# Gate products from rounded parts, with the first one-hot on Pool

## The reference

```python
cand_i = (i1[..., :, None] * N_KEYS + i2[..., None, :])
top_s, pos = lax.top_k(cand_s, PEER_TOPK)
experts = jnp.take_along_axis(cand_i, pos, axis=-1)
gates = jax.nn.softmax(top_s, axis=-1)
u = expert_down[experts]
vv = expert_up[experts]
act = jax.nn.gelu(jnp.einsum("thkd,td->thk", u, hb), approximate=False)
return jnp.einsum("thk,thkd->td", (gates * act).astype(vv.dtype), vv)
```

## Time and profile before

| | |
|---|---|
| median of 3 runs | 1893.9 us (1893.64 to 1896.47) |
| profiled execution | 1895.4 us, its span 1893.7 us |
| PE busy | 1662.7 us, 88% |
| DVE busy | 1340.0 us, 71% |
| ACT busy | 859.2 us, 45% |
| Pool busy | 231.4 us, 12% |
| mean granted TensorE clock | 0.927 |
| gate products L1407, 512 records | 67.8 us, 275 ns each |
| one-hots L1540, 256 | 55.4 us, 278 ns each |
| gated one-hots L1543, 256 | 70.9 us, 339 ns each |

### The profile page before, as it was taken

The page is one execution under the profiler, slowest core; times in us unless marked ns, Lnnn a source line. Parts: engine busy times, 40 slices in busy tenths (PEclk is TensorE's granted clock), DMA queues, the critical chain, the costliest instruction groups (busy, mean ns, idle before and its releaser), DMA issues. The chain is left out here.

```text
span 1893.7 us, 26367 instructions
## 1 busy us (share of the span) xinstructions
PE 1662.7 (88%) x10148; PEld 1500.5 (79%) x10148; DVE 1340.0 (71%) x2454; ACT 859.2 (45%) x1340; POOL 231.4 (12%) x147
## 2 busy tenths in 40 slices
PE   3998677899999999979999998999976577889988
PEld 2887666799999999968888886988756566679986
DVE  6778866588998999857777775565879435554554
ACT  3442124555545555535555554564432533355543
POOL 0301410000000000022222221100248300000000
PEclk8987889999999999989999999999987767989999
DMA  9746214366766555557777675555430000445542
GB/s 335 241 137 199 90 45 150 123 212 223 231 225 212 167 149 164 161 183 245 245 239 240 243 243 201 189 177 186 170 111 1 1 0 22 156 133 179 179 158 109
DMA packets 114946, 315.90 MB, mean 167 GB/s; under 512 B 10176, under 2 KB 10768, under 8 KB 105360
## 3 DMA queue, kind: packets, MB, share of 16 engines
q1 hardware_dynamic: 103536, 279.65, 44.7%
q10 hardware_dynamic: 10976, 33.63, 5.3%
q0 software_dynamic: 320, 1.06, 0.2%
HBM read 295.42 MB, written 18.89 MB: 166 GB/s over the span
## 5 line engine op out<-in xcount | busy, mean ns | idle before, releaser
L286 PE MATMUL ps<-parts,parts 128*128 128x512 f32 (+1 forms) x5016 | 976.4, 357 | 56.9 <-DVE parts L276 56.8
L286 PEld LDWEIGHTS ps<-parts,parts 128*128 128x128 f32 x5016 | 836.7, 193 | 195.1 <-DVE parts L276 36.1
L276 DVE TENSOR_TENSOR parts<-lead,parts 128x512 fp32r<-128x512 f32 x940 | 722.7, 780 | 339.5 <-ACT parts L271 336.1
L271 ACT CAST parts<-lead 128x512 fp32r<-128x512 f32 x940 | 581.2, 621 | 674.3 <-PE ps L286 459.8
L1421 PE MATMUL ps<-parts,parts 128*128 128x256 f32 x3072 | 385.3, 285 | 4.5 <-DVE parts L276 4.5
L1421 PEld LDWEIGHTS ps<-parts,parts 128*128 128x128 f32 x3072 | 372.6, 192 | 5.5 <-DVE parts L276 5.5
L1632 POOL TENSOR_TENSOR parts<-mem,parts 128x1024 fp32r<-128x1024 f32 x32 | 76.7, 2396 | 837.8 <-ACT parts L1614 837.8
L361 PE MATMUL ps<-lead,mem 128*128 128x128 f32 (+2 forms) x314 | 60.1, 371 | 87.7 <-ACT mem L469 49.6
L361 PEld LDWEIGHTS ps<-lead,mem 128*128 128x128 f32 (+2 forms) x314 | 52.0, 184 | 94.0 <-issue 40.6
L1543 DVE TENSOR_SCALAR mem<-lead,mem 128x128 f32<-128x128 f32 x256 | 70.9, 339 | 0.0
L1407 PE MATMUL ps<-mem 128*128 128x128 f32 x512 | 67.8, 275 | 0.7 <-DVE mem L1543 0.7
(11 more groups left out here) (327 smaller groups left out, 1196.2 us busy)
## 6 DMA issues: line engine op xcount, KB each, us to landing
lead<-in_peer_expert_down SPq DMA_DIRECT2D x64, 1024.0 KB, 5.5
lead<-in_peer_expert_up SPq DMA_DIRECT2D x64, 1024.0 KB, 5.5
lead<-in_w_in SPq DMA_DIRECT2D x50, 1024.0 KB, 5.1
lead<-in_w_ffn_in SPq DMA_DIRECT2D x22, 1024.0 KB, 5.2
act_spill<-mem ACTq DMA_DIRECT2D x32, 512.0 KB, 5.4
mem<-act_spill ACTq DMA_DIRECT2D x32, 512.0 KB, 3.5
mem<-in_w_ada SPq DMA_DIRECT2D x26, 512.0 KB, 5.6
lead<-in_w_ffn_out SPq DMA_DIRECT2D x11, 1024.0 KB, 4.8
```

The lines of the kernel that those rows point to most:

```text
L271: act.copy(w_hi[g % BUFFERS], st.words(n, u * UNIT, UNIT)).then_inc(hi_ready, 1)
L276: dve.tensor_tensor(w_lo[g % BUFFERS], st.words(n, u * UNIT, UNIT), w_hi[g % BUFFERS].bitcast(F32), ALU.subtract).then_inc(lo_ready, 1)
L286: mm = pe.matmul(o, lhs[a], rhs[b], start=start and i == 0, stop=stop and i == 2, skip_group_check=True, **kw)
```

## The change

The gate is split into a rounded upper part and its remainder (two steps on DVE, once). DVE builds the second one-hot twice, from the upper and from the lower part of the gate. PE multiplies the first one-hot, exact in the rounded type, with each, and adds both in PSUM. The first one-hot is built on Pool. The two new buffers for the lower one-hots take the place of `gate2`, which is therefore loaded later: at the start of expert-up.

```diff
@@ inversion stage, SP
                 store_gate(sp, 1, 5)
-                load_gate(sp, 1, gate2)
@@ expert-down stage, tiles
-        one1 = [at(O_ONE + i * GT * P, GT, P) for i in range(2)]
-        one2 = [at(O_ONE + 1024 + i * GT * P, GT, P) for i in range(2)]
+        one1, one2_hi, one2_lo = ([atr(o + i * GT * P, GT, P) for i in range(2)] for o in (O_ONE, O_ONE + 1024, O_GATE2))
+        gate_hi, gate_lo = atr(O_PICKS + 3 * S, S), at(O_PICKS + 4 * S, S)
@@ PE, gates(b)
-                        mm = pe.matmul(ps[:, 4 + b % 4, j * P:(j + 1) * P], one1[b % 2][:, j, :], one2[b % 2][:, j, :],
-                                       start=True, stop=True)
+                        o = ps[:, 4 + b % 4, j * P:(j + 1) * P]
+                        pe.matmul(o, one1[b % 2][:, j, :], one2_hi[b % 2][:, j, :], start=True, stop=False)
+                        mm = pe.matmul(o, one1[b % 2][:, j, :], one2_lo[b % 2][:, j, :], start=False, stop=True)
@@ Pool, new
+            @block.gpsimd
+            def _(pool):
+                pool.wait_ge(s_pt, 1)
+                for b in range(NB4):
+                    if b >= 2:
+                        pool.wait_ge(s_gm, b - 1)
+                    for j in range(GT):
+                        one = pool.tensor_scalar(one1[b % 2][:, j, :], iota, pick(0, b * GT + j), None, ALU.is_equal)
+                    one.then_inc(s_o1, 1)
@@ DVE, gated_onehots(b)
                     for j in range(GT):
-                        one = dve.tensor_scalar(one1[b % 2][:, j, :], iota, pick(0, b * GT + j), None, ALU.is_equal)
-                    one.then_inc(s_o1, 1)
-                    for j in range(GT):
-                        one = dve.tensor_scalar(one2[b % 2][:, j, :], iota, pick(1, b * GT + j), pick(2, b * GT + j),
+                        t = b * GT + j
+                        dve.tensor_scalar(one2_hi[b % 2][:, j, :], iota, pick(1, t), gate_hi[:, t:t + 1].bitcast(F32),
+                                          ALU.is_equal, ALU.mult)
+                        one = dve.tensor_scalar(one2_lo[b % 2][:, j, :], iota, pick(1, t), gate_lo[:, t:t + 1],
                                                 ALU.is_equal, ALU.mult)
                     one.then_inc(s_o2, 1)
@@ DVE, unit 161
                         dve.wait_ge(s_pt, 1)
+                        step(dve.tensor_copy(gate_hi, pick(2, 0, S)))
+                        step(dve.tensor_tensor(gate_lo, pick(2, 0, S), gate_hi.bitcast(F32), ALU.subtract))
@@ expert-up stage, SP and DVE
             def _(sp):
+                load_gate(sp, 1, gate2)
                 st.issue(sp, n_in2a[0])
...
                 dve.wait_ge(s_ld, 16)
+                dve.wait_ge(s_grow, 64)
```

## The result

The changed kernel takes 1919.35 us (median of 4 runs, 1918.85 to 1919.55), beside 1894.63 us for the kernel before: a ratio of 1.0129, 95% interval 1.0111 to 1.0146, +24.7 us. The forecast was +33 (1927), its range 1905 to 1970. The profiled execution of after has a span of 1917.1 us, 23.4 more than before.

The account below looks back on a forecast made before the run. PE bounds the gate stretch before the change, and DVE, with Pool in its way, was to become the bound: 32 + 0.7 + 0.5 = +33 on 1893.9 gives 1927 us, range 1905 to 1970.

Parts of the forecast that it names:

- PE gains nothing: Gate products: a rounded 128-column product takes 0.11 us, as 8-column products do, so PE's four-unit cycle stays 8.42 us.
- Rival (B): Gate products: rounded 128-column products stream at 512-column pace, 0.23 us each; PE's cycle 11.32, +62, 1957 us; chance 9%.
- Rival (E): Gate one-hots on DVE: second scalar costs nothing, 0.196 us per operation; 1895 us, or 1880 with faster products; chance 5%.
- DVE's own part: Gate stretch: DVE's work per four-unit cycle becomes 8.62 us, 0.20 over PE's 8.42; alone +4 us.
- Pool's cost: Gate stretch: each of 12 Pool operations per cycle delays DVE 0.11 us; with DVE's own part +32 us.
- the 0.16 row: Earlier 64-element Pool operation, blocked by DVE, ending 0.16 us after DVE did; one of two rows behind Pool's cost.
- L276 blocked as well: Gate stretch: DVE's two-tensor L276 is also held up by Pool, taking longer than its 0.69 us alone.
- Pool keeps up: Gate stretch: Pool's four operations per block, some 0.5 us each, finish in time, in a buffer free two blocks ahead.
- Pool operations over 0.6 for which PE itself waits: Gate stretch: a trace sign that would show the forecast wrong.
- The gate2 load: Start of expert-up: the moved 512 KB load delays the first act_spill load by 0 to 1.2 us, taken as +0.5.
- The two steps of the gate's split: Once on DVE: a copy of 256 elements (0.35 us) and a subtraction (less than 0.69), +0.7 us.
- The clock: Gate stretch: PE's idle time might drop its clock to 1.2 GHz, some 4.3 us per unit, beyond the range; no share.

Follow-up runs that it names:

- e3: The changed kernel, but Pool builds the first one-hot for the first two blocks only and PE reuses these: 1906.24 us, ratio 1.0069 to the kernel before.
- e5: The changed kernel without the gate's lower part, gate2 load in its old place, Pool's work unchanged: 1894.94 us, ratio 1.0001 to the kernel before.
- e4: The kernel before with only the gate2 load moved to the start of expert-up: 1893.89 us, ratio 0.9999.
- e11: The kernel before with the gate2 load and two more such loads at the start of expert-up: 1894.18 us, ratio 0.9999.
- e9: The changed kernel with Pool's four one-hots per block replaced by one two-input tensor_tensor of 512 elements: 1949.18 us, ratio 1.0287 to the kernel before.
- e2: The kernel before with only the first one-hot moved from DVE to Pool: 1895.45 us, ratio 1.0008.

## Why the prediction was right, and where it was off

- **PE gains nothing: right.** 0.11 was taken from the 8-column row; the median measured is 0.112. The Trainium skill (TensorE: Matmul & The Clock Gate, Back-to-back issue gap) gives about 81 ns at 128 columns; the traces show a median of 111 to 113 in every kernel of the study, so the measurement decides. Rival (B) hung on this pace. Rival (E) hung on a cheap second scalar, and its 1880 on the pace too; L1551 took 0.33 to 0.35 without Pool, like the old L1543.
- **DVE's own part, +4: right as the arithmetic of after**, where DVE is never idle (8.60). e3 shows that without Pool it is +8.3, since the cycle there is 0.21 longer than DVE's pure work. The prediction left this out.
- **Pool's cost, 0.11 us per operation, +28: mechanism right, size too large.** It was 0.068 by the arithmetic, +17.5, and 0.05 by e3. This is the term that was mis-sized: it was 10.5 too high, more than the 8 us by which the forecast missed, and the load that was put too low hid a part of that. The end below, 0.04, and the one above, 0.21, did enclose it. The estimate came from two meetings with Pool operations of 64 elements, of which the nearer to what was measured was the 0.16 row. So how near the total came is in part luck: two errors of opposite sign.
- **L276 blocked as well: wrong.** The prediction expected it longer than 0.69; its median is 0.679. Where the two meet here, Pool's operation becomes longer and L276 does not, so that cost falls on Pool.
- **"Pool keeps up": true by little, and for a wrong reason.** An operation was put at some 0.5 us; it takes 0.605 alone and 0.72 (e5) to 0.75 (after) on average beside DVE. Pool's need of 8.6 to 9.0 per cycle was no rival in the prediction, and e5 shows it as the bound as soon as DVE is relieved. The sign of being wrong, "Pool operations over 0.6 for which PE itself waits", came true in its first half only.
- **The gate2 load, +0.5 in a range to 1.2: mis-sized as a delay.** PE's first work came 2.1 us later, more than the bound allowed, for the first load was delayed by more than the distance between the two. In the total of e4 and e11 nothing of it could be measured; in the traces it lasts beyond the restart of PE.
- **The two steps of the gate's split, +0.7: about right.** In after's trace they hold DVE from 612.54 to 613.38, 0.84 us.
- **The clock** stayed at 1.00 (2.4 GHz) in this stretch, in e9 too, with PE busy for only 28.7 of 34 us: giving its fall no share was right.

The sum: 17.5 + 3.9 + 2.1 = 23.5, beside 23.4 between the spans and 24.7 between the medians, where 33 was forecast. That it closes to 0.1 is in part chance. By the same product of PE in both traces, after loses 21.4 us between 606 and 806 us, the two steps included, 2.3 with the start of expert-up, and -0.2 in all the rest of the span.

## What to carry to other kernels

Before splitting a short float32 product into rounded parts, read the pace of its records: at 128 columns two single products cost what one double one does, so the split buys nothing and doubles the work of the engine that makes the operands. Work moved to an idle engine must be held against the cycle as a bound of its own (operations times their pace beside the neighbour, not alone), as well as against what it costs the neighbour. When the relief of one engine shows no gain, look for the engine that is full and isn't waited for yet: e2's row had Pool at 34.00 of 34 before any experiment suffered from it. To tell which of two engines holds a third, compare when each of the two had finished with when the third began, in the same trace.

## What the runs showed of the hardware that we had not expected

- Pool beside DVE's short one-input operations costs DVE 0.05 to 0.07 us for an operation of 128 elements, 0.17 for one of 256, and 0.77 for a two-tensor one of 512, while Pool's own operation grows from 0.605 to 1.13 when it meets a 0.6 us tensor_tensor of DVE.
- Pool's one-hot of 128x128 takes 0.605 us, twice the 0.29 of the affine select of the same size.
- One transfer of 512 KB from another queue delays the first load of a stage by about 2 us (3.9 to 6.3 from issue to landing), and three of them by no more (5.8).
- The same gap of PE between two stages is followed by 2.8 to 5.9 us at a granted clock of 0.50, differently in each profile, which alone moves the time of the next 61 products by up to 1.4 us.
